# Turning the attention probabilities by VectorE and DRAM instead of TensorE

## What is computed

```python
for g, (window, dilation) in enumerate(((128, 1), (512, 4), (2048, 16))):
    scores = einsum(q, k) * head_dim ** -0.5      # banded and causal within a residue class
    m = max(scores); e = exp(scores - m); den = sum(e)
    o = einsum(e, v) / den                        # and lse = m + log(den)
att = sum(softmax(lse over groups) * o)           # merged, then gated and projected
```

## Time and profile before

| | us |
|---|---|
| median of 3 runs | 1320.94 (1320.46 to 1321.1) |
| the profiled execution | 1320.64 |
| its span, first to last instruction | 1318.6 |
| TensorE busy | 1310.0 |
| VectorE busy | 734.4 |
| ScalarE busy | 476.6 |
| GpSimd busy | 516.7 |

### The profile page before, as it was taken

The page is one execution under the profiler, slowest core; times in us unless marked ns, Lnnn a source line. Parts: engine busy times, 40 slices in busy tenths (PEclk is TensorE's granted clock), DMA queues, the critical chain, the costliest instruction groups (busy, mean ns, idle before and its releaser), DMA issues.

```text
span 1318.6 us, 17821 instructions
## 1 busy us (share of the span) xinstructions
PE 1310.0 (99%) x6070; PEld 1087.8 (83%) x6070; DVE 734.4 (56%) x1352; ACT 476.6 (36%) x1186; POOL 516.7 (39%) x500
## 2 busy tenths in 40 slices
PE   9999999999999999999999999999999999999998
PEld 6887888888888888888888888888888888888887
DVE  7799888852665665565656551266323456234323
ACT  7455655642323344243442777211100011233000
POOL 6986424404257432142240424341195316135020
PEclk9999999999999999999999999999999999999999
DMA  6232222232344454443544565385289535022111
GB/s 245 80 112 81 81 95 73 96 125 73 83 114 104 97 147 100 113 122 85 151 101 106 138 161 161 100 279 196 84 324 389 180 120 185 28 75 65 41 41 48
DMA packets 215387, 164.72 MB, mean 125 GB/s; under 512 B 116449, under 2 KB 172033, under 8 KB 215297
## 3 DMA queue, kind: packets, MB, share of 16 engines
q1 hardware_dynamic: 175008, 87.76, 24.9%
q10 hardware_dynamic: 40288, 75.82, 16.2%
HBM read 121.42 MB, written 42.09 MB: 124 GB/s over the span
## 4 chain that ended last, share of the span: by engine, by line
PE 94%; DVE 4%; ACT 1%; DMA 0%; issue 0%; SPq 0%; ACTq 0%
PE bank L1318 29%; PE bank L1323 29%; PE bank L1322 29%; PE bank L1466 2%; PE bank L1446 2%; PE bank L1455 1%; DVE xc L1048 1%; PE bank L1559 1%; PE bank L1363 0%; DVE ibuf L1075 0%; DMA gain_mix<-in_gain_mix 0%; DVE ibuf L1064 0%; DVE tbuf L1067 0%; DVE y_lo L1084 0%; ACT hn L660 0%
## 5 line engine op out<-in xcount | busy, mean ns | idle before, releaser
L599 POOL TENSOR_SCALAR ring<-raw 128x512 fp32r<-128x512 f32 x221 | 159.9, 724 | 710.1 <-PE bank L1323 549.3
L595 POOL TENSOR_TENSOR ring<-raw,ring 128x512 fp32r<-128x512 f32 x221 | 316.6, 1433 | 18.5
L1318 PE MATMUL bank<-hn,ring 128*128 128x512 f32 x640 | 252.0, 394 | 1.6 <-DVE sgbuf L1036 1.2
L1323 PE MATMUL bank<-hn,ring 128*128 128x512 f32 x640 | 249.4, 390 | 0.0
L1322 PE MATMUL bank<-hn,ring 128*128 128x512 f32 x640 | 249.0, 389 | 0.0
L1318 PE MATMUL bank<-ring,hn 128*128 128x512 f32 x576 | 232.4, 403 | 0.0
L1323 PE MATMUL bank<-ring,hn 128*128 128x512 f32 x576 | 225.5, 392 | 0.0
L1322 PE MATMUL bank<-ring,hn 128*128 128x512 f32 x576 | 225.1, 391 | 0.0
L1318 PEld LDWEIGHTS bank<-hn,ring 128*128 128x128 f32 x640 | 120.2, 188 | 27.0 <-DVE sgbuf L1036 1.6
L1323 PEld LDWEIGHTS bank<-hn,ring 128*128 128x128 f32 x640 | 120.1, 188 | 25.4
L1322 PEld LDWEIGHTS bank<-hn,ring 128*128 128x128 f32 x640 | 120.3, 188 | 24.1
(11 more groups left out here) (180 smaller groups left out, 2057.1 us busy)
## 6 DMA issues: line engine op xcount, KB each, us to landing
raw<-in_w_tail_s SPq DMA_DIRECT2D x104, 256.0 KB, 3.0
turn_dram<-qkr SPq DMA_DIRECT2D x384, 32.0 KB, 1.8
qkT<-turn_dram SPq DMA_DIRECT2D x96, 128.0 KB, 2.1
g_in<-gate_dram ACTq DMA_DIRECT2D x48, 256.0 KB, 3.7
raw<-in_w_rnn_s SPq DMA_DIRECT2D x45, 256.0 KB, 2.6
raw<-in_w_qkv_s SPq DMA_DIRECT2D x48, 192.0 KB, 2.9
gate_dram<-g_out ACTq DMA_DIRECT2D x32, 256.0 KB, 2.2
raw<-in_w_qkv_s SPq DMA_DIRECT2D x48, 128.0 KB, 2.6
```

The source lines that it names most:

```text
L595: nc.gpsimd.tensor_tensor(ring[:, ring_slot(p), 1], raw[:, p % RAW], ring[:, ring_slot(p), 0].bitcast(F32), ALU.subtract).then_inc(w_ready, 1)
L599: nc.gpsimd.tensor_scalar(ring[:, ring_slot(p), 0], raw[:, p % RAW], 1.0, 1.0, ALU.mult, ALU.mult).then_inc(hi_cut, 1)
L1318: ins = T.matmul(out, lhs[0], rhs[0], start=first, stop=False)
L1323: return T.matmul(out, lhs[1], rhs[0], start=False, stop=last)
```

## The change

Tiles are handled in pairs (2k, 2k + 1), and TensorE no longer turns probabilities.

- The masked scores and the exponentials of a pair lie side by side in bank 6 (up to 4 blocks of 128 columns), and VectorE's maximum writes there; it waits for the exponential of the tile before and, at a pair's first tile, for the turning of the last pair.
- In step 2k + 5 VectorE, at the end of its step, waits for the pair's second exponential and turns the blocks of 32 x 32 from bank 6 to `turned` in SBUF. SyncE writes them to `probs_dram` and reads them into one of two pair buffers of `probsT`. ScalarE's copy is gone.
- Queries and keys go by pairs too: four writes of 64 KB and a read of 256 KB for two tiles. SyncE does all that in odd steps, in the order: write queries and keys, write probabilities, read queries and keys, read probabilities.
- The value product moves from lag 6 to lag 8, so there are 104 steps in place of 102. `loaded_after` loads the second half of a chunk's pieces one slot later.
- `qkT` is laid out by tiles, the rotation writes directly to the pair buffer and is turned in place, and the gains of q and k have one buffer, loaded for each group.

```diff
-LAG_QK, LAG_ET, LAG_PV = 4, 5, 6
+LAG_QK, LAG_ET, LAG_PV = 4, 5, 8
+PAIRS = TILES // 2
...
-        return FIRST_QKV + KD * (c + 1) + (KD // 2 if s < 2 else KD)
+        return FIRST_QKV + KD * (c + 1) + (KD // 2 if s < 3 else KD)
...
+def columns_of(g):
+
+    return 2 if has_prev(g // (HEADS * NT), g % NT) else 1
...
+def first_column(g):
+
+    return columns_of(g - 1) if g % 2 else 0
...
+def pair_columns(k):
+
+    return columns_of(2 * k) + columns_of(2 * k + 1)
...
+            def write_qk(k):
+
+                sp.wait_ge(qkr_done, 2 * k + 2)
+                if k >= 2:
+                    sp.wait_ge(qkT_in[k % 2], 16 * (k // 2))
                 for i in range(QUADS):
-                    sp.dma_start(squares[:, :, i].rearrange("b i j -> i b j"),
-                                 qkr[i * QUAD:(i + 1) * QUAD, r].rearrange("p w a b -> p (w a b)").rearrange(
-                                     "p (b j) -> p b j", j=QUAD)).then_inc(turn_out[r], 16)
-                sp.wait_ge(turn_out[r], 16 * QUADS * (g // 2 + 1))
-                if g >= NT:
-                    old = g - NT
-                    sp.wait_ge(qk_done, old - old % NT + last_reader(old // (HEADS * NT), old % NT) + 1)
-                sp.dma_start(qkT[:, :, s * P:(s + 1) * P],
-                             squares.rearrange("(w b) i a j -> (b i) w (a j)", w=2)).then_inc(qkT_in[r], 16)
+                    sp.dma_start(turn_dram[k % 2, :, :, i].rearrange("b i j -> i b j"),
+                                 qkr[i * QUAD:(i + 1) * QUAD, k % 2].rearrange("p t c -> p (t c)").rearrange(
+                                     "p (b j) -> p b j", j=QUAD)).then_inc(turn_out[k % 2], 16)
+
+            def write_probs(k):
+
+                cols = QUADS * pair_columns(k)
+                sp.wait_ge(et_done, k + 1)
+                if k >= 2:
+                    sp.wait_ge(probsT_in[k % 2], 16 * (k // 2))
+                for i in range(QUADS):
+                    sp.dma_start(probs_dram[k % 2, 0:cols, :, i].rearrange("b i j -> i b j"),
+                                 turned[i * QUAD:(i + 1) * QUAD, 0:cols * QUAD].rearrange(
+                                     "p (b j) -> p b j", j=QUAD)).then_inc(et_out, 16)
+
+            def read_qk(k):
+
+                s = 2 * k % NT
+                sp.wait_ge(turn_out[k % 2], 16 * QUADS * (k // 2 + 1))
+                if 2 * k >= NT:
+                    old = 2 * k - NT
+                    sp.wait_ge(qk_done, old - old % NT
+                               + max(last_reader(old // (HEADS * NT), t) for t in (s, s + 1)) + 1)
+                sp.dma_start(qkT[:, s:s + 2].rearrange("p t w q -> p (t w) q"),
+                             turn_dram[k % 2].rearrange("(t b) i a j -> (b i) t (a j)", b=QUADS)
+                             ).then_inc(qkT_in[k % 2], 16)
+
+            def read_probs(k):
+
+                n = pair_columns(k)
+                sp.wait_ge(et_out, 16 * QUADS * (k + 1))
+                if k >= 2:
+                    sp.wait_ge(pv_done, 2 * k - 2)
+                sp.dma_start(probsT[:, k % 2, 0:n * P].rearrange("p (m q) -> p m q", q=P),
+                             probs_dram[k % 2, 0:QUADS * n].rearrange("(m b) i a j -> (b i) m (a j)", b=QUADS)
+                             ).then_inc(probsT_in[k % 2], 16)
...
             for what, G in MAIN_ORDER:
                 if what == "slot":
                     loaded = load_pieces(loaded, loaded_after(G))
-                elif G < TILES:
-                    turn_tile(G)
-                if (what, G) == ("step", TILES - 1):
-                    break
+                elif G % 2:
+                    k, m = G // 2, (G - LAG_ET) // 2
+                    if k < PAIRS:
+                        write_qk(k)
+                    if 0 <= m < PAIRS:
+                        write_probs(m)
+                    if k < PAIRS:
+                        read_qk(k)
+                    if 0 <= m < PAIRS:
+                        read_probs(m)
+                    if m == PAIRS - 1:
+                        break
             load_pieces(loaded, PIECES)
...
-                    nc.scalar.activation(scores[:, g % 2, c0:], scores[:, g % 2, c0:], ACT.Exp, scale=-1.0,
+                    nc.scalar.activation(scores_of(g), scores_of(g), ACT.Exp, scale=-1.0,
                                          bias=neg_max[:, col:col + 1], accum_out=den[:, col:col + 1]
...
-                g = A - LAG_ET
-                if 0 <= g < TILES:
-                    grp, tile = g // (HEADS * NT), g % NT
-                    c0 = 0 if has_prev(grp, tile) else P
-                    act.wait_ge(et_done, g + 1)
-                    if g >= 2:
-                        act.wait_ge(pv_done, g - 1)
-                    nc.scalar.activation(probsT[:, g % 2, c0:], bank[6][:, c0:2 * P], ACT.Copy).then_inc(etc_done, 1)
...
-                    if g >= 2:
-                        dve.wait_ge(et_done, g - 1)
-                    V.tensor_tensor_reduce(out=scores[:, g % 2, c0:], in0=bank[5][:, c0:2 * P],
+                    if g >= 1:
+                        dve.wait_ge(exp_done, g)
+                    if g >= 2 and g % 2 == 0:
+                        dve.wait_ge(et_done, g // 2)
+                    V.tensor_tensor_reduce(out=scores_of(g), in0=bank[5][:, c0:2 * P],
...
+                    rot = qkr[:, g // 2 % 2, g % 2]
+                    rot4 = rot.rearrange("p (w a b) -> p w a b", w=2, a=2)
...
-                    link(V.tensor_tensor(qks[:], qkn, qks[:], ALU.add))
...
+                    link(V.tensor_tensor(rot4, qkn, rot4, ALU.add))
+                    V.transpose(rot, rot).then_inc(qkr_done, 1)
+                k, odd = divmod(A - LAG_ET, 2)
+                if 0 <= k < PAIRS and not odd:
+                    dve.wait_ge(exp_done, 2 * k + 2)
+                    if k >= 1:
+                        dve.wait_ge(et_out, 16 * QUADS * k)
+                    n = pair_columns(k)
+                    V.transpose(turned[:, 0:n * P], scores[:, 0:n * P]).then_inc(et_done, 1)
...
-                    pe.wait_ge(qkT_in[g % 2], 16 * (g // 2 + 1))
+                    pe.wait_ge(qkT_in[g // 2 % 2], 16 * (g // 4 + 1))
...
-                    T.matmul(bank[5][:, 0 if prev else P:2 * P], qkT[:, 0, tile * P:(tile + 1) * P],
+                        keys = qkT[:].rearrange("p (n c) w q -> p c n w q", n=2)[:, tile % 4, :, 1]
+                    T.matmul(bank[5][:, 0 if prev else P:2 * P], qkT[:, tile, 0],
                              keys, start=True, stop=True).then_inc(qk_done, 1)
-                g = A - LAG_ET
-                if 0 <= g < TILES:
-                    grp, tile = g // (HEADS * NT), g % NT
-                    pe.wait_ge(exp_done, g + 1)
-                    if g >= 1:
-                        pe.wait_ge(etc_done, g)
-                    for b in ((0, 1) if has_prev(grp, tile) else (1,)):
-                        ins = T.transpose(bank[6][:, b * P:(b + 1) * P], scores[:, g % 2, b * P:(b + 1) * P], ident[:])
-                    ins.then_inc(et_done, 1)
                 g = A - LAG_PV
                 if 0 <= g < TILES:
                     grp, tile = g // (HEADS * NT), g % NT
                     c, vb = part_of(g // NT, 2)
-                    pe.wait_ge(etc_done, g + 1)
+                    pe.wait_ge(probsT_in[g // 2 % 2], 16 * (g // 4 + 1))
                     if g >= 1:
                         pe.wait_ge(ot_done, g)
-                    parts = (0, 1) if has_prev(grp, tile) else (1,)
-                    for b in parts:
-                        ins = T.matmul(bank[7][:, 0:P], qkv[:, c % 3, tile if b else prev_tile(grp, tile), vb],
-                                       probsT[:, g % 2, b * P:(b + 1) * P], start=b == parts[0], stop=b == 1)
+                    tiles = (prev_tile(grp, tile), tile) if has_prev(grp, tile) else (tile,)
+                    for b, t in enumerate(tiles):
+                        col = first_column(g) + b
+                        ins = T.matmul(bank[7][:, 0:P], qkv[:, c % 3, t, vb],
+                                       probsT[:, g // 2 % 2, col * P:(col + 1) * P], start=b == 0, stop=t == tile)
                     ins.then_inc(pv_done, 1)
 
             def positions(grp, tile, w):
```

More of the change, by code:

```diff
@@ L278, in build_layer @@
         qkv = at("qkv", [P, 3, NT, CHUNK, HD], F32, E)
-        qkT = at("qkT", [P, 2, S], F32, E + 49152)
+        qkT = at("qkT", [P, NT, 2, P], F32, E + 49152)
         cossin = at("cossin", [P, NT, 3, HD // 2], F32, E + 57344)
[L281 to L287, removed]
+        gain_qk = at("gain_qk", [P, 2, HD], F32, E + 63488)
+        qkr = at("qkr", [P, 2, 2, 2 * P], F32, E + 64512)
+        turned = at("turned", [P, 4 * P], F32, E + 68608)
+        probsT = at("probsT", [P, 2, 4 * P], F32, E + 70656)
+        o_buf = at("o_buf", [P, 2, 2 * P], F32, E + 74752)
+        masks = at("masks", [P, 3 * P], F32, E + 76800)
         neg_max = at("neg_max", [P, TILES], F32, E + 78336)
@@ L346, in build_layer, with scores_of @@
```

(46 more changed lines are left out.)

17 lines of the change are left out of this document (4 added, 13 removed).

## The result

The changed kernel takes **1308.93 us** (median of 4, 1307.64 to 1310.03), the kernel before 1320.86 beside it: a ratio of 0.9911 (0.9899 to 0.9923), 11.9 us faster. Forecast were 1304.7 us, within 1302 to 1315. So the direction and the range held, and 4.2 us of the gain are missing: the time lies above the 1302.5 to 1306 us of the main case, among those of the second rival (late in places, 1306 to 1315). The profiled execution is the slowest of the four, at 1310.03 us with a span of 1307.9.

What follows compares the result with a forecast made beforehand. TensorE's instruction stream was taken as the bound: from the profiled 1320.64 us, 15.4 for 140 transposes and 0.8 of waits come off, giving 1304.4, or 1304.7 us for the median of runs; range 1302 to 1315.

Steps and rivals of the forecast that it cites:

- the main case: Whole kernel: the transposes' time comes off and turned pairs arrive in time; 1304.7 us, 1302.5 to 1306; chance 0.74.
- the second rival: Round trip late only where weight burst, late exponential and slow landing meet: 1306 to 1315, say 1310 us; chance 0.10.
- The bound: Stage weaving attention into projections: TensorE's instruction stream sets the time, busy 487.20 of 487.50 us.
- the price of the transposes: TensorE's stream: 140 probability transposes at 0.11 us by distance of starts, 15.4 us off the path.
- The 0.8 us of waits: TensorE's two waits at the probability transposes, for ScalarE's exponential and copy, go too: 0.8 us gained.
- What hides VectorE's and ScalarE's edits: VectorE's 48 block transposes, at most 0.89 us each, fit its over 200 us idle; ScalarE's lost copies gain nothing.
- The round trip: Turned probabilities through DRAM: there 11.7 us after the odd step's score product (T), needed at T + 15.0 in group 0.
- its dear end: Round trip with the longest landings, 4.2 us for small writes and 3.9 for the read: T + 15.0, no slack.
- Both signs of being wrong: TensorE waiting behind the value or score product's semaphore; issues of 64 KB writes longer than 0.5 us.
- The slot of the weights: Loading the second half of a chunk's weight pieces one slot later: three slots of cover left, costs nothing.
- The rule against the change: Skill's rule wanting 128 x 128 transposes on TensorE; if it held, the time would be the slower rival's, 1341 us.
- The slower rival: Round trip late everywhere, each step growing by a quarter of the excess; 1.5 us over costs 36: 1341; chance 0.11.

Runs made afterwards that it cites:

- slot2: The changed kernel with the second half of a chunk's weight pieces loaded from the chunk's second tile on, as before the change: 1314.07 us.
- lag9_slot2: The changed kernel with the value product at lag 9 and the second half of a chunk's pieces loaded from the second tile on: 1308.38 us.
- lag7: The changed kernel with the value product one step earlier, at lag 7 in place of 8: 1384.84 us.
- spread: The changed kernel with the next chunk's weight pieces loaded one per slot in place of four at a time at two slots: 1319.47 us.

## Why the prediction was right, and where it was short

**The bound and the price of the transposes: right.** 0.11 us each against 0.106 measured, and the distances of steps fell by 0.22 in group 0. (One slip in the range: at 0.13 us each the sum gives 1301.9 us, not 1302.5.)

**The 0.8 us of waits that I added to the gain: wrong.** The two waits of the earlier trace rows belong to one step, at 732.4: ScalarE was late after a change of tables, the weight load waited for its exponential and the matmul for its copy. By starts that step was 0.6 us over its kind, and the lateness did not belong to the transposes. The value product meets it now (ScalarE's copy L852, 0.4 us, and the step at 723.9, again 0.6 us over its kind).

**What hides VectorE's and ScalarE's edits: right.** A turning of 512 columns took 0.67 us where at most 0.89 were allowed. No wait of TensorE in this stage leads to VectorE.

**The round trip: right for a typical pair, and wrong at its dear end.** T + 12.0 against T + 11.7. The step that failed is the bound: I took the longest landings of the small writes and reads, which gave T + 15.0, "just no slack", and left the issue of four writes at 1.89 us. Behind four pieces of weights the issues themselves took 4.33 us, and the value product waited until 480.69, T + 16.8. So behind a burst not only the landing is late but the issue, and with it all that SyncE has still to do. Both signs of being wrong that the prediction names came: TensorE waits at the value product, and issues of 64 KB writes last longer than 0.5 us (0.49 in the median, 2.45 at most). What came is the second rival, "late in places", which I had at 0.10 and 1310 us. The time is close to its number, but its cause is only in part the one found: a burst and slow landings are there, a late exponential is not (all four late pairs were turned by T + 4.1), and the stretched issue it did not have. So the range held through a case of chance 0.10 and not through the forecast of 0.74, which is partly luck. The 0.10 was too little: the profile before already had a burst of 4.35 us where 3.8 is usual, and writes of up to 4.2 us to land. It also had a stretched issue, right behind the burst of the earlier trace rows:

```profile
414.27 3.04 SPq L542 DMA_DIRECT2D turn_dram<-qkr  x4
```

**The slot of the weights: wrong.** I put the move at nothing because pieces still come in time. It is worth 5.1 us by `slot2`. `lag9_slot2` shows that this is for the most part turned probabilities that are late; that it is the burst's place which makes them late is argued, not shown.

**The rule against the change.** The Trainium skill ("VectorE: DVE Perf Modes", section "Rules for kernel authors") would have left the transposes on TensorE. In this kernel, with TensorE busy all through the stage, the ratio of 0.9911 decides against it; in `lag7`, the same detour with a step less, it would have been right.

**The slower rival: right in its kind, not this kernel's case.** Lag 7 shows it at work. The time is within the range given for it, but the waits are a fifth smaller than its rule says, and the lower clock makes up for that.

## What to carry to other kernels

Price an instruction that leaves the bound engine by the distance of starts, with and without it, not by its duration: here 0.11 us against 0.27. Where its work goes through a queue that carries bursts, lay out one burst case in the queue's own time, with the issues stretched as well as the landings and the loads of other queues beside it, and give the consumer a step of slack if it costs no buffer: one step of lag was worth 2.8 us here, and one too few cost 76. Before a load is moved, look for who else stands in the order of the engine that takes it.

## What the runs showed of the hardware that was not expected

The issue of a DMA is not a constant: four writes of 64 KB in runs of 128 B took 1.96 us in a quiet queue, as much as four of 32 KB (1.89). Right behind 1 MB of weights they took 2.1 to 3.1 us at ten places and 4.33 and 4.00 at two, where ScalarE's queue had issued 0.4 MB as well. The Trainium skill ("DMA: Bandwidth & Descriptors", section "Anatomy of one DMA — SWDGE (gpsimd) path", which is on the path of another engine) says that many descriptors can be emitted before their cost shows; the quiet case agrees, with twice the descriptors in the same time. The burst is another matter, since the writes behind it are no larger.

TensorE's clock goes with its waits. In `spread` TensorE was busy for 3.17 of the 6 us from 431 to 437, and in the next 6 us the granted clock was 0.51, the lower of its two levels, 1.2 GHz; a distance of ordinary matmuls was 0.43 us there in place of 0.23. In the changed kernel, with single waits of 1.5 us at most, it stayed at 1.00.
